# Order of work between the SSD heads and the RWKV heads: exponents ahead of the state copy, decay logits and sums ahead of a projection, a constant moved into the exp

## The reference, cut to what matters

```python
# SSD: 8 heads; a = dt * a_neg, cum = cumsum(a) in a chunk
decay = exp(where(causal, cum[..., :, None] - cum[..., None, :], -inf))
y = einsum('bhcts,bhcsp->bhctp', scores * decay, xdt) + (cm * exp(cum)) @ state
# RWKV: the decay of each token, and the unit key
z = rw_w0[d] + tanh(low) @ rw_w2[d]
w = exp(-0.606531 * sigmoid(z))
kk = k * rw_kk;  kk = kk * rsqrt(sum(kk * kk) + 1e-12)
# RWKV values: v = centred token shift of the projected columns
out = rows + mu[0] * (prev - rows) + mu[1] * (nxt - rows)
```

## Time and profile before

| What | Value |
|---|---|
| Median of 3 runs | 1397.25 us (1395.37 to 1403.73) |
| The profiled execution: time, and span of its trace | 1397.81 us, 1396.0 us |
| Mean granted TensorE clock | 0.985 |
| TensorE matmul busy | 1292.2 us, 93% |
| VectorE busy | 379.4 us, 27% |
| ScalarE busy | 223.0 us, 16% |
| GpSimd busy | 50.1 us, 4% |
| Read from HBM | 451.79 MB, 324 GB/s over the span |

### The profile page before, as it was taken

One profiled execution on the slowest core, in us unless ns is written; L12 is line 12 of the kernel. 1 busy time (PEld: TensorE's weight loads), 2 busy tenths in 40 slices (PEclk: granted clock), 3 DMA queues, 4 the chain that ended last, 5 costly groups with the idle time before them and its releaser, 6 DMA issues.

```text
span 1396.0 us, 21253 instructions
## 1 busy us (share of the span) xinstructions
PE 1292.2 (93%) x9112; PEld 606.4 (43%) x9112; DVE 379.4 (27%) x915; ACT 223.0 (16%) x447; POOL 50.1 (4%) x81
## 2 busy tenths in 40 slices
PE   5999999967789999999999999999999999999997
PEld 2555466657678533333333333333333333333333
DVE  0214526865533221112111211121111211121112
ACT  2332212353331310001000000000000100010001
POOL 0002100052100000000000000000000000000000
PEclk9999999989999999999999999999999999999999
DMA  9464430130305899999999999999999999999994
GB/s 391 188 232 160 180 129 1 61 122 5 123 4 207 346 424 427 428 427 427 428 428 428 428 428 428 428 428 428 428 427 428 427 428 427 427 427 427 428 427 173
DMA packets 33482, 453.96 MB, mean 325 GB/s; under 512 B 3744, under 2 KB 4000, under 8 KB 4352
## 3 DMA queue, kind: packets, MB, share of 16 engines
q1 hardware_dynamic: 33408, 452.86, 77.4%
HBM read 451.79 MB, written 1.05 MB: 324 GB/s over the span
## 4 chain that ended last, share of the span: by engine, by line
PE 75%; DMA 12%; DVE 8%; issue 2%; ACT 2%; SPq 0%; DVEq 0%
PE PS L1800 72%; DMA arena<-in_moe_w_gu 10%; DMA arena<-in_ada_first 2%; PE PS L2555 1%; DVE arena L1694 1%; DVE arena L1225 1%; DVE arena L1700 1%; DVE arena L1697 1%; DMA arena<-in_ada_rest 1%; PE PS L2546 1%; DVE arena L1693 0%; PE PS L2209 0%; PE PS L1812 0%; DVE arena L1375 0%; DVE arena L1470 0%
## 5 line engine op out<-in xcount | busy, mean ns | idle before, releaser
L1800 PE MATMUL PS<-arena 128*64 128x512 f32 (+9 forms) x8746 | 1243.3, 424 | 60.7 <-DMA arena<-in_ada_first 17.0
L1800 PEld LDWEIGHTS PS<-arena 128*64 128x64 f32 (+5 forms) x8746 | 565.2, 148 | 686.2 <-issue 613.5
L1693 DVE TENSOR_SCALAR arena<-PS 128x256 f32<-128x256 f32 x64 | 38.6, 603 | 512.4 <-PE PS L1800 512.4
L1071 ACT ACTIVATE arena<-arena 128x256 f32<-128x256 f32 x64 | 26.7, 417 | 485.7 <-DVE arena L1693 485.7
L1722 DVE TENSOR_TENSOR arena<-PS,arena 128x512 f32<-128x512 f32 x32 | 22.2, 693 | 217.4 <-PE PS L1800 217.4
L1081 ACT COPY arena<-PS 128x256 f32<-128x256 f32 x32 | 11.9, 373 | 303.7 <-PE PS L2546 303.7
L2555 PE MATMUL PS<-arena 128*128 128x128 f32 x128 | 26.3, 287 | 32.2 <-DVE arena L1700 32.2
L2555 PEld LDWEIGHTS PS<-arena 128*128 128x128 f32 x128 | 14.4, 142 | 58.5 <-DVE arena L1700 42.4
L1694 DVE TENSOR_SCALAR arena<-PS 128x256 f32<-128x256 f32 x64 | 39.1, 611 | 0.0
L1481 DVE COPY arena<-PS 128x384 f32<-128x384 f32 (+2 forms) x48 | 23.1, 488 | 54.4 <-PE PS L1800 54.4
L1225 DVE SCALAR_TENSOR_TENSOR arena<-PS,arena 128x255 f32<-128x255 f32 (+5 forms) x68 | 32.7, 481 | 13.4 <-ACT arena L840 11.1
(11 more groups left out here) (243 smaller groups left out, 391.1 us busy)
## 6 DMA issues: line engine op xcount, KB each, us to landing
arena<-in_moe_w_gu SPq DMA_DIRECT2D x128, 2048.0 KB, 25.5
arena<-in_moe_w_down SPq DMA_DIRECT2D x64, 2048.0 KB, 26.7
arena<-in_ada_rest SPq DMA_DIRECT2D x16, 1024.0 KB, 7.3
arena<-in_w_in SPq DMA_DIRECT2D x5, 2048.0 KB, 8.5
arena<-in_ada_first SPq DMA_DIRECT2D x4, 2048.0 KB, 14.3
arena<-in_w_out SPq DMA_DIRECT2D x4, 1024.0 KB, 5.9
arena<-in_tokens SPq DMA_DIRECT2D x1, 2048.0 KB, 20.9
arena<-in_consts SPq DMA_DIRECT2D x1, 1536.0 KB, 31.5
```

What stands on the lines that cost most here:

```text
L1071: act.activation(sgm[:, 256 * half:256 * half + 256], glu[:, 256 * half:256 * half + 256], ACT.Sigmoid, scale=ALPHA).then_inc(sig_ready, 1)
L1693: dve.tensor_scalar(by_rest(glu), of_half(0), LIMIT, None, ALU.min).then_inc(glu_ready, 1)
L1800: ins = pe.matmul(out, lhsT, rhs, start=start, stop=stop, skip_group_check=skip)
```

## The change

The exponents of heads 0 and 1 run on VectorE ahead of the copy of the state. On TensorE `decay_logits(1)` and `running_sums(2)` stand ahead of the second half of the projection of `rv`, and the first matmul of `ra` gives back the projection's weight buffer. The shift of `rv` on VectorE moves from q = 1 to q = 2, behind the weights of heads 4 and 5. The product of `lw` with -0.606531 is dropped; its sigmoid itself signals `lw_ready`, and the three exps of each `decays` carry the constant as their scale. `ssd_variance()` stands between the two `scale_by_decays(0, d)`.

```diff
@@ scalar engine
-                    act.activation(lw, lw, ACT.Sigmoid).then_inc(rz_sig, 1)
+                    act.activation(lw, lw, ACT.Sigmoid).then_inc(lw_ready, 1)
...
-                step(act.activation(eb[d][:, 0, :, :], cu[:, 0, :, :], ACT.Exp))
-                step(act.activation(eb[d][:, 1, :, :], cu[:, 0, :, :], ACT.Exp, scale=-1.0))
-                Q.drained(name, act.activation(eb[d][:, 2, :, :], cu[:, 1, :, :], ACT.Exp))
+                step(act.activation(eb[d][:, 0, :, :], cu[:, 0, :, :], ACT.Exp, scale=-DECAY))
+                step(act.activation(eb[d][:, 1, :, :], cu[:, 0, :, :], ACT.Exp, scale=DECAY))
+                Q.drained(name, act.activation(eb[d][:, 2, :, :], cu[:, 1, :, :], ACT.Exp, scale=-DECAY))
@@ vector engine
-            R.arrived(dve, "st")
-            R.drained("st", dve.tensor_copy(Sst, pair("st").rearrange("p (a b) -> p a b", a=2)))
...
+            exponents(0)
+            exponents(1)
+            R.arrived(dve, "st")
+            R.drained("st", dve.tensor_copy(Sst, pair("st").rearrange("p (a b) -> p a b", a=2)))
             dve.wait_ge(conv_silu, 4)
             for q in range(4):
                 if q:
                     dve.wait_ge(w_ready, 2 * q)
-                exponents(2 * q)
-                exponents(2 * q + 1)
-                if q:
+                    exponents(2 * q)
+                    exponents(2 * q + 1)
                     gather_heads(q - 1)
                 weights(2 * q)
                 weights(2 * q + 1)
...
-                if q == 1:
+                if q == 2:
                     shift("rv", 4, (vT[:, 0, :], P, NT), (vT[:, 1, :], P, NT))
-                if q == 2:
                     R.arrived(dve, "rkn")
                     R.drained("rkn", dve.tensor_scalar(kk.rearrange("p a b -> p (a b)"), pair("rkn"), 1e-12, None, ALU.add))
-                    dve.wait_ge(rz_sig, 1)
-                    dve.tensor_scalar(lw, lw, -DECAY, None, ALU.mult).then_inc(lw_ready, 1)
...
-            ssd_variance()
             for d in range(2):
                 scale_by_decays(0, d)
+                if d == 0:
+                    ssd_variance()
@@ tensor engine
             running_sums(1)
             R.emptied(pe, "st")
             head_pair(0)
-            project_in("rv", 1)
             decay_logits(1)
             running_sums(2)
+            project_in("rv", 1)
             head_pair(1)
             R.claim(pe, "ra")
             for c in range(2):
                 ins = mm(pair("ra")[:, 512 * c:512 * c + 512], W2A[64:96, c * P:c * P + P], lowT[64:96, :])
+                if c == 0:
+                    pay(ins)
```

More of the change, by code:

```diff
@@ L457, in hybrid_block @@
         lv_arg, lv_exp, lk_ready, level_half, gsq_ready, gn_std, gla_done = named("lv_arg lv_exp lk_ready level_half gsq_ready gn_std gla_done")
-        rw_tanh, rz_sig, lw_ready, kk_sq, rw_pre, gate_sig = named(
-            "rw_tanh rz_sig lw_ready kk_sq rw_pre gate_sig")
+        rw_tanh, lw_ready, kk_sq, rw_pre, gate_sig = named(
+            "rw_tanh lw_ready kk_sq rw_pre gate_sig")
         rw_in, squares_ready, cat_ready, ssd_done = named("rw_in squares_ready cat_ready ssd_done")
```

## The result

| | Before | Changed |
|---|---|---|
| Median | 1399.67 us (1395.37 to 1405.22, 14 runs) | 1405.9 us (1402.88 to 1414.08, 14 runs) |
| Profiled execution, span | 1396.0 us | 1401.1 us |
| Ratio to before | | 1.0042, 95% interval 1.0029 to 1.0056 |

The change costs 0.42%, 4 to 8 us of 1400. It is slower, by less than the 1% of the prediction's bound.

The account below looks back on a forecast made before the run. DMA engines full during the experts, so the end follows the mixer. Squares +5.6 (301.4), `sn` and variance 2.85, second scaling 1.7 give 305.9 against 301.6: +4.3 us, 1397.81 to 1402.1, median 1401.5; range 1396 to 1408.

Parts of the forecast that it names:

- End moves with the mixer: Experts behind the mixer: DMA engines are full, so any shift of the mixer reaches the kernel's end one for one.
- Hoist, constant: 0: First exponents ahead of the state copy, and the 128x2048 product dropped on VectorE: each worth 0.
- The 4.5 us wait becomes one of 6.9 elsewhere: VectorE's 4.51 us wait for `rz1` is replaced by 6.9 us before the gather of head pair 1.
- TensorE idle 8.1 us at `rkn`, released by the shift: TensorE waits 8.1 us at `rkn` until the later shift of `rv` frees its banks, at 278.2.
- Clock behind the gap: Behind TensorE's gap at 1.2 GHz: `rkn` takes 3.4 us instead of 1.75, sums 3 3.3 instead of 2.8.
- Head pair 3 to end 43.3 behind head pair 0: TensorE's head pair 3, second half after VectorE's weights 6 and 7 at 293.6, ends at 296.0.
- One blocked step at the squares, 2.4: VectorE's gated product and squares meet GpSimd's last two products: 2.4 us lost, bounds 0 and 2.4.
- Variance inside the wait for `sn`: 1.1: First scaling moves ahead of the variance, into VectorE's 2.17 us wait for `sn`: a gain of 1.1.
- Second scaling: 1.7, bounds 1.3 to 2.0: Second `scale_by_decays` on VectorE beside GpSimd: 1.7 us, where it took 2.0.
- Squares at 48.7, M 53.2: Counted from head pair 0's end: squares end (301.4) and M, the second `scale_by_decays(0, d)` end (305.9).
- the clock again: Rival: TensorE's thin work behind head pair 3 puts the first doublings at 1.2 GHz; +8, 1405; chance 0.1.
- the strict reading: Port shared by VectorE and GpSimd locked exclusively for a whole instruction; the sum would be 1 to 2 us worse.

Follow-up runs that it names:

- e6: Changed kernel plus 30 unread 128x128 matmuls on TensorE ahead of its wait for the banks of `rkn`; 1401.23 us, ratio to before 0.9999.
- e4: Changed kernel with TensorE's order and the place of the `rv` shift put back as before; 1399.86 us, ratio to before 0.9986.
- e1: Changed kernel with `rkn` moved from bank group 0 to group 1 in the table; 1399.97 us, ratio to before 0.9989.
- e2: Kernel before with only the shift of `rv` moved from q = 1 to q = 2; 1406.32 us, ratio to before 1.0043.
- the second profile: Changed kernel run and profiled once more, nothing altered; 1407.05 us, ratio to before 1.0041.
- e9: e7 with GpSimd's last two 128x1024 products of the keys made by VectorE instead; 1393.27 us, ratio to before 0.9960.
- e5: Changed kernel with `ssd_variance` ahead of both `scale_by_decays` again; 1408.65 us, ratio to before 1.0050.
- e7: Changed kernel with `rkn` in bank group 1 and head pair 1 ahead of the second half of `rv`; 1398.83 us, ratio to before 0.9980.

## Why the prediction was right

The range (1396 to 1408) held the time, and the sign, the place and the mechanism came out. By its own steps:

- *End moves with the mixer.* Yes: DMA share 1.01 over the experts as before, and M's +4.0 to +4.9 comes out at the end as +6.2 with an interval of 4 to 8. The other kernels follow as well: M from 42.7 to 55.9, medians from 1392.9 to 1408.7, nearly in the order of M. The exception is e6, with M 2.6 us over before and a ratio of 0.9999.
- *Hoist, constant: 0.* Yes, up to the squares (e4); behind them no difference that runs could tell (0.9986, with 1 inside the interval).
- *The 4.5 us wait becomes one of 6.9 elsewhere.* 6.95.
- *TensorE idle 8.1 us at `rkn`, released by the shift.* 8.19 from the last matmul of `ra`, 8.2 in the waits; the bank is the cause (e1), the move of the shift is the edit that makes it so (e2).
- *Clock behind the gap.* Yes for `rkn`: 3.7 us against 2.0 at full clock, a loss of 1.7 where 1.65 was priced (3.4 against 1.75); shown by e6. No for sums 3: they took 2.8 us as before, the lower of the two bounds, not 3.3, since the clock was full again; the second profile has 3.1.
- *Head pair 3 to end 43.3 behind head pair 0* (296.0): 42.4. Of the 0.9, 0.6 is there already at the end of head pair 2 (35.4, not 36.0), most of it the 0.5 of sums 3. The rest is GpSimd: its first two instructions took 1.50 us together, not 2.19, and it was done with its three steps at 287.16, 36.2 behind head pair 0 and not 36.8, so VectorE's weights hardly waited for it.
- *One blocked step at the squares, 2.4.* Gated product and squares took 4.8 us for what took 2.6: 2.2. Shown by e9, where these and the two products of the keys take 1.2 each.
- *Variance inside the wait for `sn`: 1.1.* In sign; e4 shows 1.6 with what else lay there, e5 2.2 against the profile with the same clock at `sn`, 1.1 of it the first scaling.
- *Second scaling: 1.7, bounds 1.3 to 2.0.* No: 2.4, beside GpSimd; 1.2 in the second profile.
- *Squares at 48.7, M 53.2.* 47.8 and 52.87. That M is so close is in part luck: the 0.9 that the squares came earlier and the 0.7 that the second scaling took longer nearly cancel, and the second profile has 53.75.

Two sizes were off. The base: the first three runs of before had a median of 1397.25, fourteen have 1399.67, and that alone is 2.4 of the 4.4 us between 1401.5 and 1405.9. The rest, 6.2 against 4.3, lies inside the interval; e6 hints that part of it is the clock behind M, a small form of the rival "the clock again", but no run separates it. The Trainium skill's rule on the shared port ("SBUF — State Buffer", "SBUF: two separate sides"): the strict reading was priced 1 to 2 us worse than my sum, and the time of the blocked step came out within 0.2 of the milder one. The rows of e7 and e9 agree with an exclusive lock where both engines multiply tensors, at 3.25 against 1.23 us.

## What to carry to other kernels

A read that is moved later frees its banks later: look up who claims them next, and count from the end of the last read, not from the work itself. When banks are handed round by a table, the entry is as much a part of the order as the code. A gap on TensorE can cost again behind itself (here 1.7 us at `rkn`), and moving one engine's long products beside another's can cost as much (here 2.2 us).

## What the runs showed of the hardware

Thirty matmuls that nobody reads, in a gap of 8 us, kept the granted clock at 1.00 over `rkn` behind it, where it was 0.52; 3.7 us became 2.0. A VectorE product of two 128x1024 tensors in SBUF took 3.25 us beside GpSimd's product and 1.23 without, and GpSimd's own product took 3.21 instead of 2.36: the squares started at 295.52 and ended 1.1 us after GpSimd's product did (297.70). They took turns, and both paid. And of two kernels with a difference of 1.6 us in M (before and e4) timed runs could tell nothing (0.9968 to 1.0004), while the profile's M repeated to 0.01 us for the kernel before, but only to 0.9 for the changed one, where `sn` ran at full clock in one profile (2.1 us) and at the 1.2 GHz level in the other (3.8 us).
